# A recurrent scan whose last row group is finished in the next solve stage, with the projection products between its chunks dealt out by a table over three PSUM banks

## What is computed

```python
def step(S, inp):
    r_t, w_t, k_t, v_t, kk_t, a_t = inp
    sa = jnp.einsum('bhij,bhj->bhi', S, -kk_t)
    S = (S * w_t[:, :, None, :] + sa[..., :, None] * (kk_t * a_t)[..., None, :]
         + v_t[..., :, None] * k_t[..., None, :])
    return S, jnp.einsum('bhij,bhj->bhi', S, r_t)
...
y = ((y - mu) * lax.rsqrt(var + GN_EPS)).reshape(B, T, RWKV_WIDTH) * P['rwkv_gn_g'][l] + P['rwkv_gn_b'][l]
bonus = jnp.sum(r * k * P['rwkv_r_k'][l].reshape(H, N), axis=-1, keepdims=True) * v
return y + bonus.reshape(B, T, RWKV_WIDTH), S_fin, p_shift[:, -1:]
...
merged = (gA * ((yA * jax.nn.silu(zA)) @ P['w_br_rwkv'][l]) ...
```

## Time and profile before

| | us |
|---|---|
| median of 3 runs (4593.88 to 4602.98) | 4594.7 |
| the profiled execution's own time | 4594.06 |
| its span, first to last instruction | 4592.2 |
| TensorE busy | 4269.3 (93%) |
| VectorE busy | 2283.7 (50%) |
| ScalarE busy | 1629.7 (35%) |
| GpSimd busy | 815.5 (18%) |
| DMA, mean share of 16 engines | 17.8% |
| granted TensorE clock, mean | 0.976 |

### The profile page before, as it was taken

How to read it: one execution, slowest core, us unless ns; L and a number is a source line. 1 busy time by engine, 2 the same in 40 slices (tenths; PEclk the granted TensorE clock), 3 DMA queues, 4 the chain that set the end, 5 groups by cost and what they waited for, 6 DMA issues and landing times. The chain is left out here.

```text
span 4592.2 us, 74574 instructions
## 1 busy us (share of the span) xinstructions
PE 4269.3 (93%) x29488; PEld 2991.4 (65%) x29488; DVE 2283.7 (50%) x4732; ACT 1629.7 (35%) x3886; POOL 815.5 (18%) x980
## 2 busy tenths in 40 slices
PE   7999998989999989999979999989899999899999
PEld 4666665567766667777446656655676666677774
DVE  3666663346624454534435665634566245535344
ACT  4333433355623432122043334334556244311220
POOL 0011010000010024543300110100000100245433
PEclk9999999999999999999989999999999999999999
DMA  5010012010021122321250100120100211223222
GB/s 204 19 36 15 32 27 84 19 30 18 12 92 53 58 76 93 108 93 66 88 199 23 32 15 32 27 84 17 32 18 12 92 59 52 76 93 108 93 77 79
DMA packets 129148, 280.76 MB, mean 61 GB/s; under 512 B 30041, under 2 KB 55897, under 8 KB 123554
## 3 DMA queue, kind: packets, MB, share of 16 engines
q1 hardware_dynamic: 128802, 275.99, 17.8%
HBM read 230.96 MB, written 42.62 MB: 60 GB/s over the span
## 5 line engine op out<-in xcount | busy, mean ns | idle before, releaser
L1063 PE MATMUL banks<-hT,w_piece 128*128 128x384 f32 x1536 | 536.7, 491 | 0.2
L1063 PEld LDWEIGHTS banks<-hT,w_piece 128*128 128x128 f32 x1536 | 276.3, 190 | 161.1 <-issue 6.5
L2265 PE MATMUL banks<-hT,w_piece 128*128 128x384 f32 x1056 | 354.1, 489 | 1.4 <-ACT sb_gate_raw L2375 1.4
L2265 PEld LDWEIGHTS banks<-hT,w_piece 128*128 128x128 f32 x1056 | 196.1, 190 | 141.4 <-issue 16.6
L2721 DVE TENSOR_TENSOR gate_quarters<-gate_kept,banks 128x288 f32<-128x288 f32 x144 | 65.4, 454 | 296.0 <-PE banks L2584 291.0
L2672 ACT ACTIVATE gate_kept<-banks 128x288 f32<-128x288 f32 x144 | 59.1, 410 | 429.9 <-PE banks L2584 429.9
L2721 DVE TENSOR_TENSOR branch_quarters<-branch_kept,banks 128x288 f32<-128x288 f32 x144 | 65.4, 454 | 264.9 <-PE banks L2584 264.8
L2434 DVE TENSOR_TENSOR pass<-pass,constants 128x128 f32<-128x128 f32 x128 | 41.2, 322 | 311.8 <-ACT take L2386 309.3
L2437 DVE TENSOR_TENSOR_SCAN left<-pass,zero 128x384 f32<-128x384 f32 (+7 forms) x144 | 190.5, 1323 | 5.0
L1023 POOL TENSOR_TENSOR state_decayed<-state,decay_of_chunk 128x128 f32<-128x128 f32 x120 | 86.1, 717 | 532.5 <-DVE state L1301 532.5
L2030 DVE SCALAR_TENSOR_TENSOR keysT<-banks,gains,rstd 64x128 f32<-64x128 f32 (+1 forms) x272 | 112.1, 412 | 98.5 <-ACT rstd L1940 93.3
(11 more groups left out here) (428 smaller groups left out, 9814.0 us busy)
## 6 DMA issues: line engine op xcount, KB each, us to landing
w_piece<-in_w_cols SPq DMA_DIRECT2D x66, 512.0 KB, 4.4
w_ada<-in_w_ada SPq DMA_DIRECT2D x24, 1024.0 KB, 9.5
w_gate_ahead<-in_w_cols SPq DMA_DIRECT2D x48, 512.0 KB, 4.4
w_branch<-in_w_br SPq DMA_DIRECT2D x96, 256.0 KB, 2.8
w_gate<-in_w_cols SPq DMA_DIRECT2D x48, 512.0 KB, 4.3
y_branch<-y_gated SPq DMA_DIRECT2D x12, 1152.0 KB, 7.8
sb_cached_keysT<-in_sbkT SPq DMA_DIRECT2D x8, 1024.0 KB, 7.7
sb_cached_values<-in_sbv SPq DMA_DIRECT2D x8, 1024.0 KB, 5.1
```

The costliest lines, as they stand in the source:

```text
L1063: last = mm(dst, w[0 if kind in ("k", "v") else 1][:, k, :], hT[:, k, c], start=(k == 0), stop=(k == KD - 1))
L2265: last = mm(ps[:, bank[n], 0:TG], w_of[wn][:, k, :], hT[:, k, TG * g:TG * g + TG], start=(k == 0), stop=(k == KD - 1))
```

## The change

It has two parts.

**1. The last row group goes to the next solve stage.** In a fused stage with preparation (h = 0, 1, 2) the roots, norm, transposes, gate and store of group 3 are left out; only its sums stay. The statistics tile is kept over stages (R.st). The next solve has them: on ScalarE the logarithm and exponential ahead of its first copies; on VectorE the norm ahead of the first masks and the gate behind them; on TensorE two transposes into bank 2 behind the first products; on SyncE the store, behind three loads. The store of group 2 now stands behind the state halves and is the one whose landing the fused stage does not wait for; y_tail counts two stores for each head pair (y_tails 16 to 32). The loads of the head parameters and of k_shifted stand behind the store.

**2. Fills by a table.** FILL_END = 4 becomes FILL_ENDS, one number for each chunk, 65 in all instead of 64; fill_chunk sums it up. In a scan stage nine groups (k1 to v0) go round banks 0, 1 and 7 instead of 0 and 1, with a semaphore free7.

```diff
-FILL_LEAD, FILL_MID, FILL_END = 24, 1, 4
+FILL_LEAD, FILL_MID = 24, 1
+FILL_ENDS = (6, 3, 4, 4, 3, 3, 5, 6, 3, 5, 4, 4, 4, 3, 4, 4)
...
     end = sum(FILL_SIZE[:n + 1]) - FILL_LEAD
-    return -1 if end <= 0 else min(NCK, -(-end // (FILL_MID + FILL_END)) - 1)
+    chunk = -1
+    while end > 0 and chunk < NCK:
+        chunk += 1
+        end -= FILL_MID + FILL_ENDS[chunk] if chunk < NCK else end
+    return chunk
...
-            fill_bank = [0, 1, 2, 3, 0, 1, 3] + [x % 2 for x in range(len(FILL) - 7)]
+            fill_bank = [0, 1, 2, 3, 0, 1, 3] + [(0, 1, 7)[x % 3] if 7 + x < FILL_AT["v", 1] else x % 2 for x in range(len(FILL) - 7)]
...
-                fill(end)
+                fill(ends[n])
                 if n == 10:
                     pe.wait_ge(y_normed, 2)
+                    if prep:
+                        pe.wait_ge(free[7], fill_bank.count(7))
...
             fill(1000)
-            pe.wait_ge(y_normed, 4)
-            turns(3, 4)
+            if not prep:
+                pe.wait_ge(y_normed, 4)
+                turns(3, 4)
```

SyncE at the end of the fused stage, and in the solve:

```diff
-                for q in range(3):
+                for q in range(2):
                     sp.wait_ge(y_gated, q + 1)
                     sp.dma_start(yg[0, h, :, span(q)], out[:, span(q)]).then_inc(y_stored, 16)
...
                 sp.wait_ge(s_scaled, NCK + 2)
                 for hh in range(2):
                     hc = slice(64 * hh, 64 * hh + 64)
                     sp.dma_start(O["wkv_p"][l, h, hc], ST[hc, hc]).then_inc(state_out, 16)
-                sp.wait_ge(y_gated, 4)
-                sp.dma_start(yg[0, h, :, span(3)], out[:, span(3)]).then_inc(R.y_tail if prep else y_stored, 16)
+                sp.wait_ge(y_gated, 3)
+                sp.dma_start(yg[0, h, :, span(2)], out[:, span(2)]).then_inc(R.y_tail if prep else y_stored, 16)
...
                 sp.wait_ge(state_out, 48)
-                sp.wait_ge(y_stored, 48 if prep else 64)
+                sp.wait_ge(y_stored, 32 if prep else 64)
...
+            def store_tail():
+                sp.wait_ge(tail_gated, 1)
+                sp.dma_start(yg[0, before, :, tail_cols], T_.kT[:, tail_cols]).then_inc(T_.y_tail, 16)
```

TensorE, ScalarE and VectorE in the solve stage (tail is h >= 1):

```diff
             scores(0)
             rows(0)
+            if tail:
+                pe.wait_ge(tail_normed, 1)
+                for x, i in enumerate(range(first_row, end_row)):
+                    last = nc.tensor.transpose(tail_bank[:, P * x:P * x + P], Z[:, i, :], ident)
+                last.then_inc(tail_turned, 1)
...
+            if tail:
+                sg, own = T_.st[:, 2 * first_row:2 * end_row], InOrder(act, act_own)
+                own(copy(sg, sg, ACT.Ln, scale=1.0 / 64, bias=con("eps")[:, 1:2]))
+                copy(sg, sg, ACT.Exp, scale=-0.5).then_inc(tail_rooted, 1)
             rows(0)
...
+            if tail:
...
+                dve.wait_ge(tail_rooted, 1)
+                own(V.tensor_tensor(Yg, Yg, sg, ALU.mult), tail_normed)
             for k in (0, 2, 3, 4, 1):
                 mask(0, k)
+            if tail:
+                out_rows, par = T_.kT[:, tail_cols], T_.par[before % 2]
+                dve.wait_ge(tail_turned, 1)
+                own(V.scalar_tensor_tensor(out_rows, tail_bank, par[:, 8:9], T_.bonus[before % 2][:, tail_cols], ALU.mult, ALU.add))
+                own(V.scalar_tensor_tensor(out_rows, out_rows, par[:, 9:10], T_.zs[before % 2][:, tail_cols], ALU.add, ALU.mult), tail_gated)
```

More of the change, by code:

```diff
@@ L489 @@
     Z: object
+    st: object
     kT: object
@@ L496, with load_first @@
     ends: object
-def load_first(sp, A, l, con, R, h, nx, sem, tails=0):
+def load_first(sp, A, l, con, R, h, nx, sem, tails=0, store_tail=None):
     n = 0
     if nx is not None:
-        for dst, src in ((R.par[nx % 2][:, 0:10], A["rw_par"][l, nx]), (R.wl[:, :], A["w_lora"][l, nx]), (R.w[0][:, :, :], A["w_cols"][l, G_K + nx]),
-                         (R.w[1][:, :, :], A["w_cols"][l, G_R + nx])):
+        for dst, src in ((R.wl[:, :], A["w_lora"][l, nx]), (R.w[0][:, :, :], A["w_cols"][l, G_K + nx]), (R.w[1][:, :, :], A["w_cols"][l, G_R + nx])):
             sp.dma_start(dst, src).then_inc(sem, 16)
             n += 16
+        if store_tail is not None:
+            store_tail()
         if tails:
             sp.wait_ge(R.y_tail, tails)
-        sp.dma_start(R.kT[:, :], con("reset")).then_inc(sem, 16)
-        n += 16
+        for dst, src in ((R.kT[:, :], con("reset")), (R.par[nx % 2][:, 0:10], A["rw_par"][l, nx])):
+            sp.dma_start(dst, src).then_inc(sem, 16)
+            n += 16
         for j in range(3):
@@ L573, in rwkv_solve @@
         G = [xg[:, P:3 * P].rearrange("p (h n) -> p h n", h=2) for xg in XG]
+        tail, before = h >= 1, h - 1
+        first_row, end_row = Y_GROUPS[3]
+        tail_cols = slice(P * first_row, P * end_row)
+        tail_bank = ps[:, 2, P:P + P * (end_row - first_row)]
         @block.sync
         def _(sp):
-            sp.wait_ge(first_loaded, load_first(sp, A, l, con, T_, h, nx, first_loaded, tails))
+            def store_tail():
+                sp.wait_ge(tail_gated, 1)
+                sp.dma_start(yg[0, before, :, tail_cols], T_.kT[:, tail_cols]).then_inc(T_.y_tail, 16)
+            sp.wait_ge(first_loaded, load_first(sp, A, l, con, T_, h, nx, first_loaded, tails, store_tail if tail else None))
             if nx is None:
@@ L925, in rwkv_fused @@
         elif scan:
-            fill_bank = [0, 1, 2, 3, 0, 1, 3] + [x % 2 for x in range(len(FILL) - 7)]
+            fill_bank = [0, 1, 2, 3, 0, 1, 3] + [(0, 1, 7)[x % 3] if 7 + x < FILL_AT["v", 1] else x % 2 for x in range(len(FILL) - 7)]
         else:
-            fill_bank = [x % len(free) for x in range(len(FILL))]
+            fill_bank = [x % 6 for x in range(len(FILL))]
         turn_of = [fill_bank[:x].count(b) for x, b in enumerate(fill_bank)]
-        lead, mid, end = (FILL_LEAD, FILL_MID, FILL_END) if prep else (GATE_LEAD, GATE_MID, GATE_END)
+        lead, mid, ends = (FILL_LEAD, FILL_MID, FILL_ENDS) if prep else (GATE_LEAD, GATE_MID, (GATE_END,) * NCK)
         behind = 5 if prep else 2
@@ L988, in _ @@
                 sp.dma_start(O["wkv_s"][l, h], SN[:, :]).then_inc(state_out, 16)
-                for q in range(3):
+                for q in range(2):
                     sp.wait_ge(y_gated, q + 1)
                     sp.dma_start(yg[0, h, :, span(q)], out[:, span(q)]).then_inc(y_stored, 16)
-                    if q == 1 and not prep:
-                        for i in range(2):
-                            sp.wait_ge(g_made, NTG * (i + 1))
-                            sp.dma_start(zg[i], t[i][:, :]).then_inc(g_stored, 16)
+                if not prep:
+                    for i in range(2):
+                        sp.wait_ge(g_made, NTG * (i + 1))
+                        sp.dma_start(zg[i], t[i][:, :]).then_inc(g_stored, 16)
                 sp.wait_ge(s_scaled, NCK + 2)
@@ L1209, in _ @@
                     ACTE.activation(Y[64:P, i, :], ps[64:P, ub + 1, 0:P], ACT.Copy).then_inc(y_copied, 1)
-                if scan and n in (4, 8, 13, 16):
+                if scan and n in ((4, 8, 13) if prep else (4, 8, 13, 16)):
                     q = (4, 8, 13, 16).index(n)
@@ L1317, in _ @@
                             dve.wait_ge(fill_ready, FILL_AT["ss", g] + 1)
[L1318 removed]
+                            own(V.tensor_scalar(t[0][:, cols(g)], fill_dst(FILL_AT["ss", g]), 1e-24, None, ALU.max), maxed if g == NTG - 1 else None)
                             V.engine_nop().then_inc(free[fill_bank[FILL_AT["ss", g]]], 1)
@@ L1350, in _ @@
                     gate(2, 7)
-                if scan and n in (5, 10, 14, 16):
+                if scan and n in ((5, 10, 14) if prep else (5, 10, 14, 16)):
                     norm((5, 10, 14, 16).index(n))
@@ L1356, in _ @@
                     gate(1, 7)
-            if scan:
+            if scan and not prep:
                 gate(3, 4)
```

36 lines of the change are left out of this document (21 added, 15 removed).

## The result

The changed kernel takes 4568.83 us (median of 4 runs, 4564.5 to 4571.51); the kernel before, with a run taken beside it, 4594.29 (4 runs, 4590.0 to 4602.98). The ratio is 0.9944, 95% interval 0.993 to 0.9958: faster by 0.56%. The forecast was 4568.5, in a range of 4555 to 4579. The profiled execution took 4571.08 and its span is 4569.2, mean granted clock 0.974.

A forecast was written before the change was run, and what follows sets the result against it. TensorE's list was taken to bound the fused stage, so time comes only from its waits: 6 x (3.31 + 1.09 - 0.05) = 26.1 us off 4594.06 gives 4567.96, median 0.6 above, so 4568.5; range 4555 to 4579.

The forecast's parts named there:

- Table: Moving fills between a fused stage's chunks, to where VectorE is long, shortens chunk-to-chunk time by 3.31 us per stage.
- the four with three fills: Chunks 1, 4, 5 and 13 of a fused stage: 3.55 us instead of 4.19, saving 2.56 in all.
- Chunk 6: Fused-stage chunk with five fills: VectorE's reduction of the ss products sets 5.51 us against 5.47, losing 0.04.
- Chunk 8: Fused-stage chunk with three fills: VectorE gets the roots late behind ScalarE's copies; 3.99 us, saving 0.23 instead of 0.64.
- Tail: From the last chunk's state update (T) to the solve: last landing at T + 8.4, solve at 8.95, saving 1.09 us per stage.
- Stages: Length of each of six fused stages with scan: 3.31 us saved between chunks plus 1.09 at the end.
- Solve: The last row group's work added to the next solve is mostly covered by waits: 0.05 us each, bounds 0 and 1.9.
- Clock: TensorE's clock in solves behind scans still falls after the idle stretch: nothing gained, bounds -1.6 and +0.4 us each.
- The first rival: At the fused stage's end the landing does not bind and removed work counts in full: about 4551 us, chance 0.10.
- The second rival: In the fused stage's chunks the table only moves the waits, so the 3.31 us go: 4588 us, chance 0.08.
- the third: Slower: the clock does not come back in the solves behind scans, total 4636 us, chance 0.04.

## Why the prediction was right

The time (4568.5 against 4568.83) is closer than the terms are, and that is luck: the table gave 0.27 us a stage more than forecast and the tail 0.27 less, 1.6 us over six stages either way, and single runs lie up to 4 us from the median. The mechanism of both terms was right, as the traces show.

- **Table: 3.31 forecast, 3.58 measured** (and by the table alone the same 3.58). Chunks 0, 7, 9, 10, 11 and the four with three fills came as worked out (5.51, 5.81, 4.87, 4.63, 4.38, 3.53 to 3.58). Chunk 6 took 5.57 and not 5.51, and it would have taken 5.98 without bank 7, to which the prediction gave no worth there ("yet VectorE sets chunk 6"). Chunk 8 was the miss: 3.68, not 3.99. VectorE did wait 0.73 for the roots, as forecast, and L1373 began 7.70 after the T of chunk 7 (7.77 forecast); but it took 1.42 and not the 1.70 that I read from the earlier trace rows with its gap. In the kernel before it took 1.66 for the same shape; what goes with that stands below the list. The run with v's copy behind the roots, in which the product is 1.66 again, says that the order cost 0.1 in all.
- **Tail: 1.09 forecast, 0.82 measured.** The mechanism was right: landings end it, bound to the issue of v's shift rows in chunk 14. The sizes: the last landing that the stage waits for, the second state half, comes 8.4 to 9.1 after T, mean 8.8, and not 8.4 (0.40 behind group 1's store, itself 0.24 later than in the kernel before); and the solve follows 0.44 to 0.46 behind it and not 0.55. That distance is the same in all 30 such stages of the five kernels whose solve waits for these landings, while the solve stands anywhere from 8.7 to 10.8. In the changed kernel each later landing at the stage's end came after those issued before it. By the Trainium skill, DMA: Bandwidth & Descriptors, section Queues, rings and completion order, the write that tells of a completion lands only after the earlier writes of its DMA engine; the trace agrees. In five other traces two neighbours change places in one stage, by 0.02 to 0.11 us, which that rule for single engines leaves room for.
- **Stages: 4.07 each in the sum of their lengths**, against 4.40 forecast, which the chunks and the tail indeed gave (3.58 + 0.82): two of the six have a stretch of 3.4 us at the 1.2 GHz level at their start, +1.7 us each, where one had it before.
- **Solve: +0.05 forecast, about +0.3 to 0.4 at half clock** (58.54, 58.55 and 58.51 where 58.23, 58.12 and 58.13 stood), one pair equal (58.32 and 58.31); the last two pairs differ in how long the clock was down. In the three slower ones VectorE's first mask starts 1.00 or 1.01 after the solve does (1.40, 1.02 and 0.89 before). The half-clock stretch begins 1.2 to 1.3 us into the solve now, and from 0.1 before it to 0.6 into it then; whether that makes the difference or the tail's work does wasn't tried.
- **Clock: nothing forecast, nothing seen**: 0.94 to 0.97 in these solves, as before.
- **The first rival** (the landing does not bind) was wrong of this change, and its working was right of the kernel that lacks the slow stores: solve at 6.83 worked out, 6.88 measured, "the clock might stay up" 9 us more, of which its sum took 4: the solves behind scans are 7.2 us shorter in all (342.8 against 350.0), four of the six at 1.00. Forecast for it 4551, measured 4545.
- **The second rival** (the table only moves the waits) fell with the table alone, 4571.1 and not 4588; the third (the clock does not come back) with the clock of 0.94 to 0.97 in the solves.

The product of chunk 8 is the step with the largest miss among the chunks. GpSimd's decay of the state, in the kernel before and in the changed one:

```profile
264.75 0.40 POOL L1023 TENSOR_TENSOR state_decayed<-state,decay_of_chunk 128x128 f32<-128x128 f32 x1 [5.40 <-DVE state L1301]
```

```profile
264.93 0.40 POOL L1067 TENSOR_TENSOR state_decayed<-state,decay_of_chunk 128x128 f32<-128x128 f32 x1 [5.40 <-DVE state L1348]
```

Both stand 7.05 after the T of chunk 7. VectorE's product began 7.00 after it in the kernel before, so GpSimd's instruction fell inside; now it begins at 7.70, when that is over. In the twelve traces here the product stands 96 times: 24 times with the whole 0.40 of a GpSimd instruction inside it, each 1.66 long, and 72 times with nothing of GpSimd's inside, each 1.42. The prediction moved the product to 7.77 and kept the length that it had beside GpSimd's instruction.

What the prediction did not see is that the cause of the landing time could be moved. It took the "over 8 us" of the stores before the state halves as given, where it came from two stores of 4.5 KB together.

## What to carry to other kernels

When a stage's end waits for landings, don't look at how large the last stores are but at what was issued ahead of them: here two stores in very small pieces held everything behind them, and moving them to where nobody waits gave 23 us, nearly as much as the whole change. By the traces 17 of them are the stages and 7 the clock of the solves behind them, which stays up behind the shorter pause in four of six. Where two bounds stand close together, the gain comes only when both are gone: here one gave 0.2 us, the other nothing, both 2.6. And one run speaks for putting slow stores beside long instructions and not beside a stretch of a thousand short ones, where the instructions themselves may come late. Last, look what GpSimd does beside a VectorE instruction before you carry its length to another place: here it was 1.66 us or 1.42.

## What was not expected of the hardware

The two stores write 4 and 32 bytes per partition. Alone on the queue, the last of their 288 packets (256 pieces, and 32 more of 4 bytes) is moved 1.1 us after the second is issued, at some 0.01 us each, and still the completions come 6.5 and 7.9 us after the issues; over all runs it is 4.5 to 8.7 us for the 0.5 KB and 6.3 to 10.4 for the 4 KB, wherever in the program they stand. A store of 192 KB with nothing of the kind ahead of it lands in 1.8. The Trainium skill, DMA: Bandwidth & Descriptors, section Anatomy of one DMA, gives some 2.0 us of fixed cost for a transfer of any size, for DMAs that GpSimd issues; SyncE issues these. The 1.8 us rows lie near it and the shift rows' don't.

Open: whether it is the size of the pieces (both slow stores have small ones, and no run stored the same rows in larger pieces), what in the completion takes the time, and why they took some 0.7 us more on one of the chips.
